# The entry into a split-precision FFN: low weight products by token tile, and a second block in the other order

## The reference, cut to what matters

```python
def conv_ffn(h, w_up, conv_w, conv_b, w_down):
    S = h.shape[1]
    u = h @ w_up
    gate, val = u[..., :D_FF], u[..., D_FF:]
    gp = jnp.pad(gate, ((0, 0), (CONV_WIDTH - 1, 0), (0, 0)))
    conv = conv_b
    for i in range(CONV_WIDTH):
        conv = conv + conv_w[i] * gp[:, i:i + S]
    return (jax.nn.gelu(conv, approximate=True) * val) @ w_down
...
        x = x + rmsnorm(m, norm_mix_post[layer])
        f = conv_ffn(rmsnorm(x, norm_ffn_pre[layer]), ffn_w_up[layer], ffn_conv_w[layer],
                     ffn_conv_b[layer], ffn_w_down[layer])
        x = x + rmsnorm(f, norm_ffn_post[layer])
```

## Time and profile before

| | |
|---|---|
| median of 3 runs | 1254.26 us (1254.19 to 1254.31) |
| the profiled execution | 1254.17 us |
| its span, first to last instruction | 1252.4 us |
| TensorE's mean granted clock | 0.998 of full |
| PE busy | 1241.8 us |
| DVE, ACT, POOL busy | 809.8, 694.5, 143.7 us |

### The profile page before, as it was taken

The page is one execution under the profiler, slowest core; times in us unless marked ns, Lnnn a source line. Parts: engine busy times, 40 slices in busy tenths (PEclk is TensorE's granted clock), DMA queues, the critical chain, the costliest instruction groups (busy, mean ns, idle before and its releaser), DMA issues.

```text
span 1252.4 us, 19297 instructions
## 1 busy us (share of the span) xinstructions
PE 1241.8 (99%) x7554; PEld 1117.4 (89%) x7554; DVE 809.8 (65%) x1233; ACT 694.5 (55%) x994; POOL 143.7 (11%) x178
## 2 busy tenths in 40 slices
PE   9999999999999999999999999999999999999997
PEld 8888888888889999999998888888999999999996
DVE  5566656766678556666666877677565566565554
ACT  6444345555556655555555756555675557565554
POOL 1000002200001000000000311422001500101400
PEclk9999999999999999999999999999999999999999
DMA  9544443655553544444452655555353453363331
GB/s 339 197 164 165 169 168 134 243 202 183 187 193 132 188 152 152 152 146 135 149 173 102 246 203 180 199 175 189 109 197 124 144 194 104 133 203 117 136 135 51
DMA packets 33847, 208.55 MB, mean 167 GB/s; under 512 B 3985, under 2 KB 4258, under 8 KB 16226
## 3 DMA queue, kind: packets, MB, share of 16 engines
q1 hardware_dynamic: 31986, 201.32, 46.3%
q0 software_dynamic: 1488, 5.78, 1.3%
q10 hardware_dynamic: 288, 0.27, 0.1%
HBM read 206.30 MB, written 1.05 MB: 166 GB/s over the span
## 4 chain that ended last, share of the span: by engine, by line
PE 93%; DVE 2%; ACT 2%; issue 1%; DMA 1%; POOL 0%; SPq 0%; DVEq 0%; POOLq 0%; ACTq 0%
PE pair L593 18%; PE pair L595 17%; PE pair L594 17%; PE pair L735 12%; PE pair L729 6%; PE bank L593 3%; PE bank L594 3%; PE bank L595 3%; PE bank L1030 1%; PE bank L1055 1%; PE bank L1038 1%; PE bank L848 1%; ACT whi L1451 1%; PE bank L1005 1%; PE bank L801 1%
## 5 line engine op out<-in xcount | busy, mean ns | idle before, releaser
L1967 DVE TENSOR_TENSOR wlo<-raw,whi 128x2048 fp32r<-128x2048 f32 (+5 forms) x208 | 431.8, 2080 | 212.9 <-ACT whi L1451 212.0
L1451 ACT ACTIVATE whi<-raw 128x2048 fp32r<-128x2048 f32 (+5 forms) x208 | 361.9, 1742 | 193.7 <-PE pair L595 167.6
L593 PE MATMUL pair<-whi,bhi 128*128 128x384 f32 (+3 forms) x528 | 189.3, 359 | 0.2 <-DVE blo L2616 0.2
L595 PE MATMUL pair<-whi,blo 128*128 128x384 f32 (+3 forms) x528 | 183.7, 348 | 0.0
L594 PE MATMUL pair<-wlo,bhi 128*128 128x384 f32 (+3 forms) x528 | 183.7, 348 | 0.0
L593 PE MATMUL pair<-whi,ahl 128*128 128x384 f32 (+3 forms) x416 | 153.4, 369 | 0.5 <-DVE wlo L1967 0.5
L735 PE MATMUL pair<-ahl,whi 128*128 128x512 f32 x640 | 153.2, 391 | 0.0
L594 PE MATMUL pair<-wlo,ahl 128*128 128x384 f32 (+3 forms) x416 | 149.1, 358 | 0.0
L595 PE MATMUL pair<-whi,ahl 128*128 128x384 f32 (+3 forms) x416 | 149.0, 358 | 0.0
L735 PEld LDWEIGHTS pair<-ahl,whi 128*128 128x128 f32 x640 | 117.5, 188 | 22.6
L593 PEld LDWEIGHTS pair<-whi,bhi 128*128 128x128 f32 x528 | 100.9, 191 | 9.6 <-DVE blo L2616 0.9
(11 more groups left out here) (322 smaller groups left out, 1910.3 us busy)
## 6 DMA issues: line engine op xcount, KB each, us to landing
raw<-wstream_d SPq DMA_DIRECT2D x136, 1024.0 KB, 4.9
raw<-wstream_d SPq DMA_DIRECT2D x56, 768.0 KB, 4.2
raw<-wstream_d SPq DMA_DIRECT2D x4, 832.0 KB, 4.3
raw<-wstream_d SPq DMA_DIRECT2D x4, 800.0 KB, 4.9
gain_row<-rows_d POOLq DMA_DIRECT2D x5, 512.0 KB, 4.1
arena<-mem_d POOLq DMA_DIRECT2D x2, 1024.0 KB, 6.8
raw<-wstream_d SPq DMA_DIRECT2D x4, 384.0 KB, 3.0
raw<-wstream_d SPq DMA_DIRECT2D x4, 288.0 KB, 2.7
```

The costliest lines, as they stand in the source:

```text
L593: pe.matmul(out_ap, lhi, rhi, start=first, stop=False, skip_group_check=True)
L595: return pe.matmul(out_ap, llo, rhi, start=False, stop=last, skip_group_check=True)
L1451: act.activation(whi[:, n % RING, 0:width[n]], raw[:, n % RAW, 0:width[n]], ACT.Copy).then_inc(hi_ready, 1)
L1967: dve.tensor_tensor(wlo[:, n % RING, 0:width[n]], raw[:, n % RAW, 0:width[n]], whi[:, n % RING, 0:width[n]].bitcast(F32), ALU.subtract).th ...
```

## The change

The first block of each FFN is now written out in `first_tile`. There is no filler ahead of token tile 1. As soon as ACT has copied tile 0's part of a feature tile (128 columns, signal `tile_hi`), PE multiplies it with the low weights; the second tile's transposes stand between these, then the second tile's low products, and the high products of both tiles (512 columns) follow, alternating with what is left of the low ones. So the first block's low products are 32 of 128 columns in place of 16 of 256. ACT copies 16 times 128 columns in place of 8 times 256, first all of tile 0 and then all of tile 1, and it does so before the split of the second block's weight chunk, which stood ahead of the copies. DVE's list is the same. The second block, `second_tile`, does its high products first and then the low ones, with `spread_rows` in the middle of the low ones. All other blocks are unchanged.

```diff
-            def up_tile(held=None, between=(), merged=True):
+            def first_tile():
                 p = begin_block("v")
-                between = list(between)
+                c = w.chunk
+                slot = c % RING
+                first_hi = w.at("tile")
+                w.up("tile", KD)
+                def turn_row(t, k):
+                    added(t, k)
+                    mm = pe.transpose(bank[:, k // 2, (k % 2 * NT + t) * P:(k % 2 * NT + t + 1) * P], x[:, t, k * P:(k + 1) * P], ident[:, :])
+                    if k % 2:
+                        mm.then_inc(turned if t else tile_turned, 1)
+                def low_part(t, k):
+                    if t:
+                        high_row(k)
+                    else:
+                        pe.wait_ge(tile_hi, first_hi + k + 1)
+                    tk = slice(t * P, (t + 1) * P)
+                    for f in range(2):
+                        sl = slice((2 * k + f) * P, (2 * k + f + 1) * P)
+                        pe.matmul(pair[:, p, f, SEQ + t * P:SEQ + (t + 1) * P], wlo[:, slot, sl], ahi[:, k, tk],
+                                  start=t == 0 and k == 0, stop=False, skip_group_check=True)
+                def high_part(k):
+                    low_row(k)
+                    both = ahl[:, k, :, :].rearrange("p c s -> p (c s)")
+                    for f in range(2):
+                        sl = slice((2 * k + f) * P, (2 * k + f + 1) * P)
+                        mm = pe.matmul(pair[:, p, f, :], whi[:, slot, sl], both, start=False, stop=k == KD - 1, skip_group_check=True)
+                    if k == KD - 1:
+                        mm.then_inc(chunk_used, 1)
+                keep_warm(bank[:, 0, 0:P], 4)
+                for k in range(KD):
+                    turn_row(0, k)
+                w.up("turn", KD // 2)
+                w.up("row", KD // 2)
+                pe.wait_ge(lo_ready, c + 1)
+                for k in range(4):
+                    low_part(0, k)
+                for k in (0, 2, 4):
+                    turn_row(1, k)
+                    turn_row(1, k + 1)
+                    if k < 4:
+                        low_part(0, 4 + k)
+                        low_part(0, 5 + k)
+                low_part(1, 0)
+                low_part(1, 1)
+                turn_row(1, 6)
+                turn_row(1, 7)
+                low_part(1, 2)
+                for k in range(KD):
+                    high_part(k)
+                    if k + 3 < KD:
+                        low_part(1, k + 3)
+                w.chunk += 1
+            def second_tile():
+                p = begin_block("v")
+                c = w.chunk
+                slot = c % RING
+                pe.wait_ge(hi_ready, c + 1)
+                for k in range(KD):
...
+                        pe.matmul(pair[:, p, f, :], whi[:, slot, sl], both, start=k == 0, stop=False, skip_group_check=True)
+                pe.wait_ge(lo_ready, c + 1)
+                for k in range(KD):
...
+                        mm = pe.matmul(pair[:, p, f, SEQ:2 * SEQ], wlo[:, slot, sl], ahi[:, k, :], start=False, stop=k == KD - 1, skip_group_check=True)
+                    if k == 3:
+                        spread_rows()
...
             def ffn(l):
-                held = []
-                turn_rows(added, (4, 9, 0), held=held)
                 base = w.at("gv")
+                first_tile()
+                second_tile()
                 for j in range(UPS + 1):
-                    if j < UPS:
-                        up_tile(held[0] if j == 0 else None)
-                        up_tile(between=() if j else [nothing, nothing, spread_rows], merged=j < UPS - 1)
+                    if 0 < j < UPS:
+                        up_tile()
+                        up_tile(merged=j < UPS - 1)
...
             def ffn(l):
+                gain = COLS["norm_ffn_pre"] + l * KD
+                first, second = slice(0, P), slice(P, SEQ)
+                for k in range(KD):
+                    if k % 2 == 0:
+                        act.wait_ge(tile_turned, w.up("tile"))
+                    act.activation(ahi[:, k, first], bank[:, k // 2, k % 2 * SEQ:k % 2 * SEQ + P], ACT.Copy,
+                                   scale=cols[:, gain + k:gain + k + 1]).then_inc(tile_hi, 1)
+                for k in range(KD):
+                    if k % 2 == 0:
+                        act.wait_ge(turned, w.up("turn"))
+                    act.activation(ahi[:, k, second], bank[:, k // 2, k % 2 * SEQ + P:(k % 2 + 1) * SEQ], ACT.Copy,
+                                   scale=cols[:, gain + k:gain + k + 1]).then_inc(turned_hi if k % 2 else row_hi, 1)
                 split_hi(w.chunk - 2)
-                rows_out([(ahi, 0)], [COLS["norm_ffn_pre"] + l * KD], True)
                 row_squares(added)
                 catch_up()
```

More of the change, by code:

```diff
@@ L331, in hybrid_stack @@
         row_hi, row_lo = sem("row_hi"), sem("row_lo")
+        tile_turned, tile_hi = sem("tile_turned"), sem("tile_hi")
         rstd_step = sem("rstd_step")
@@ L706, in up_tile @@
+            def up_tile(merged=True):
+                p = begin_block("v")
                 c = w.chunk
@@ L708, in up_tile @@
                 slot = c % RING
[L709 to L724, removed]
                 if merged:
@@ L739, in up_tile @@
                         mm.then_inc(chunk_used, 1)
-                    if k % 2 and between:
-                        between.pop(0)()
                 w.chunk += 1
```

## The result

The changed kernel takes 1256.18 us (median of 20 runs, 1255.71 to 1256.86) against 1254.05 us (20 runs, 1253.68 to 1254.56) of the kernel before on the same chip: ratio 1.0017, 95% interval 1.0010 to 1.0024. It is 2.1 us slower. The profiled execution took 1256.11 us with a span of 1254.3. The forecast was 1257.2, from 1.47 us lost in each FFN; the trace has 1.05.

A forecast was written before the change was run, and what follows sets the result against it. PE, 99% busy, was taken as the bound, with a slackless ACT/DVE chain behind it. PE's 0.66 lateness plus a 0.9 stall, against the old 0.11, made 1.47 an FFN, 2.9 in all: 1257.2 us, own range 1256.2 to 1258.2, overall 1255.2 to 1263.2.

The forecast's parts named there:

- A: The forecast: PE pays 0.66 in its own order, then stalls for ACT's delayed chain; 1.47 an FFN, 1257.2 us; chance 0.45.
- The stall: PE's wait at the second tile of the first to_model: near 0.9 us, where it was 0.11.
- The narrow product: First block's 128-column low products: 0.114 us each, 32 costing 3.65 us against 1.9, 1.75 more.
- The switches: PE changing between transposes and products in the first block: two or three extra switches at 0.09 us.
- PE's second block: Start of each FFN's second block on PE: 217.13, 0.66 us later than 216.47.
- ACT's release: ACT free after its 16 row copies at 212.76; the split then is extra, the next split ends 1.78 us late.
- POOL doesn't join: POOL's two roots after the squares: some 2 us, done near 219, ahead of spread_rows at 221.74.
- B: Rival: narrow products cost 0.22 us like plain f32, second block 4.2 later, 1262.5 us; chance 0.27.
- C: Rival: narrow products cost 0.065 us by columns, chain still 0.96 late, +1.9, 1256.2 us; chance 0.15.
- D: Rival: the serial chain holds at least 0.9 us unseen that absorbs the lateness; +1.1, 1255.4 us; chance 0.10.
- E: Rival: C and D together, 2 x -0.65, 1253.0 us, the only case below the present time; chance 0.03.
- The clock: PE's clock should stay at its high level, with no gap over 1 us in the new order.

The follow-up runs named there:

- e3: Kernel before with the second block's high products first and ACT's weight split moved behind the row copies, products still 256 columns: 1257.03 against 1254.1 us.
- e4: Changed kernel with ACT's two squares of x moved behind the split of the third chunk: 1254.94 against 1254.1 us of the kernel before.
- e9: Changed kernel with ACT's squares last and the cross copy of block 1 ahead of gelu 0: 1253.97 against 1253.95 us of the kernel before.
- e1: Kernel before with each of the first block's 16 low products cut into two of 128 columns in place: 1257.25 against 1254.1 us.
- e5: Changed kernel with the second block's weight split put back ahead of ACT's 16 narrow copies: 1258.12 against 1253.93 us of the kernel before.
- e10: Changed kernel with four feature tiles cut, second block's split halved, squares last, cross copy of block 1 ahead of gelu 0: ratio 0.9991 to the kernel before.
- e8: Kernel before with ACT's cross copy of block 1 and the fifth chunk's high split ahead of gelu 0: 1256.09 us, ratio 1.0016.
- e12: e8 with DVE waiting for POOL's gate scaling before the fifth chunk's low split: 1255.49 against 1253.95 us of the kernel before.
- e6: Changed kernel with ACT's cross copy of block 1 and the fifth chunk's high split ahead of gelu 0: 1256.37 against 1253.93 us of the kernel before.

## Why the prediction was nearly right, by its steps

- **The mechanism, A, held.** PE pays its own order first and then waits at the second tile of the first to_model for a chain that ACT's late split has delayed. e3 has the chain without PE's share (31.19 for 29.66), e4 shortens it and the time follows (1.2 us), and in e9 the wait is gone and so is the loss. The stall was forecast at 0.9 and is 0.98, but that this agrees is luck: the chain was forecast 0.4 too late and PE ahead of it 0.47 too late (0.66 for 0.19), and the stall is the difference of the two.
- **The narrow product** (0.114) is 0.107 among transposes and other narrow products and 0.115 between high ones. That is the 0.11 of one pass over 64 columns, and hardly less than the 0.12 of 256 columns, as the forecast had read the 64-column row. The Trainium skill ("TensorE: Matmul & The Clock Gate", LDWEIGHTS) has 128/1.2 = 107 ns for the load of 128 columns, and the trace's 0.107 agrees. Its 81 ns for 128 columns in a stream (the same page, back-to-back issue gap) the trace doesn't reach; by that figure, as an estimate, 32 products would take 0.8 us less than at 0.107.
- **The switches** (0.26 in the sum up to 212.02, and 0.09 more in the 0.32 that it gives low(1,2)) are nothing. From the second tile's first transpose to the first high product the trace has 8 transposes and 14 narrow products in 2.34 us (209.32 to 211.66), 0.106 each; the forecast had 2.85 (209.49 to 212.34). Of these 0.51 the switches are 0.35, the narrow products 0.10 and the transposes 0.05. The five steps behind came as forecast (3.43), the last three high pairs 0.05 slower. The 0.20 of the one pair in the earlier trace rows does not recur in the new order, where four such groups can be read. A price from a single pair should have had zero as its lower bound.
- **PE's second block** therefore comes 0.22 late and not 0.66, and this is the step that failed: a term of the sum too large, above all the switches, and not its direction.
- **ACT's release** was put at 212.76, in the time of the kernel before; it is 212.20 + 0.18 = 212.38. The cause is the same: ACT starts its copies when forecast (207.85 + 0.18 = 208.03 for 208.01), but the last transposes that it follows end at 211.24 + 0.41 + 0.18 = 211.83, not 212.2. A copy is 2.01/8 = 0.25 for the first tile (0.26 forecast) and 0.29 for the second, where it waits for transposes. From there the chain was right to 0.1: 1.07 late at the conv where the forecast had 1.47 with a release 0.38 later. In e3 the release was the forecast's, and the conv was 1.52 late.
- **The sum.** 1.05 an FFN for 1.47, 2.1 for 2.9. With 0.107 and no switches the prediction's own arithmetic gives ACT's release about 0.4 earlier, 1.47 - 0.4 = 1.07 an FFN, and 1256.4. The measured 1256.18 is at the low end that A was given (1256.2), where copies and products at their cheap ends had been put; taken against the 1254.05 measured beside it, the 2.13 us stand against a forecast of 2.9 with a range of 1.9 to 3.9. The verdict that I had held most likely, 0.60 on slower by over 0.2%, did not come. The line is at 1256.8: the forecast's centre stood only 0.4 above it, and the over-sized terms were enough to cross it.
- **POOL doesn't join:** right, its roots were done at 217.50 + 0.55 = 218.05, ahead of spread_rows at 221.09, 1.9 us after the last square (216.18). But the "some 2 us" had nothing to stand on: in the kernel before the same stretch took 4.8 us (215.02 to 219.84), because POOL stood beside DVE's splits (below). From the forecast's 216.9 that would have been 221.7, just at its spread_rows.
- **The rivals.** B and C fell with e1. The time alone would not have told: C's forecast was 1256.2, nearer to the measured 1256.18 than A's centre. D (a hidden 0.9 in the chain) fell with the 0.98 wait, and with e3. E needed both.
- **The clock** stayed at 2.4 GHz in the kernel after (granted 1.00 in every stretch of both entries, also behind the 0.98 wait), as forecast; e5 is the case where it didn't.

## What to carry to other kernels

When a step is moved on an engine that seems to have time, follow what is queued behind it to the point where the bound engine next waits for that queue; here 1.8 us of split on ACT were free at their old place, cost 0.9 us at their new one, and the loss went only when the same engine was reordered once more. Cutting a product by tile doubles its weight loads: at 128 columns half a product costs nine tenths of a whole one, so cut only as many as fill the wait (four feature tiles did better than eight, 29.30 against 29.76 at the second tile, though e10 also splits its weight chunk in halves). And reordering one engine can start another's long operation beside a third's short one: look at who runs beside whom.

## What the runs showed of the hardware

- A 128-column product with rounded operands takes 0.107 to 0.115 us, a 256-column one 0.12 and a 512-column one 0.228; between transposes and such products there is no cost of changing over.
- POOL's 128x256 multiply goes from 0.74 to 2.71 us when DVE's 128x2048 subtraction of two SBUF tensors starts 0.18 ahead of it (e8), and is back at 0.73 when DVE is made to wait (e12). The same shows where I had not looked for it: POOL's root step on one column, beside DVE's split in the kernel before, took 2.18, and in the kernel after, where DVE's split comes earlier or later, 1.24 and 0.19. The first two rows are of the kernel before, which the prediction had passed over as "some 2 us":

```profile
214.09 2.18 POOL L494 TENSOR_SCALAR stat<-stat 128x1 f32<-128x1 f32 x1 [2.32 <-ACT xn L1472]
...
217.00 2.21 POOL L494 TENSOR_SCALAR stat<-stat 128x1 f32<-128x1 f32 x1
```

```profile
214.15 2.29 DVE L2043 TENSOR_TENSOR wlo<-raw,whi 128x2048 fp32r<-128x2048 f32 x1 [0.35 <-ACT whi L1516]
...
215.25 1.24 POOL L495 TENSOR_SCALAR stat<-stat 128x1 f32<-128x1 f32 x1 [3.66 <-ACT xn L1537]
...
217.22 0.19 POOL L495 TENSOR_SCALAR stat<-stat 128x1 f32<-128x1 f32 x1
```

The second fence is the timeline of the kernel after: the 1.24 ends at 216.49, when DVE's split has ended at 216.44, and the 0.19 has no split beside it. Who starts first seems to count: POOL's next step (128x2) and DVE's next split both start at 218.03 in the kernel after, and POOL takes 0.23; in e6 POOL starts it at 218.08, 0.01 after the split, and takes 2.38.
- In one FFN of e5 a wait of 1.2 us of TensorE, and some 1.8 us of transposes and narrow products behind it, were followed by some 6.8 us at 1.2 GHz; in the other FFN the same wait and the same work were not, nor were the waits of 1.50 us in e3.
